# A hybrid decoder block on one core: the order of the mixer's work, with the convolution's mean behind the second pair's state chain, taps of two blocks in turns, and fillers shifted by one place

## The reference, cut to what matters

```
h = rmsnorm(x, norm_mix_g); proj = h @ w_in
u_conv, u_rw, gate_logits = split(proj)

def conv_branch(u, dw, dw_b, ln_g, ln_b, pw, pw_b):
    a, b = split(u, 2); glu = a * sigmoid(b)
    y = depthwise causal convolution of glu, 31 taps, + dw_b
    mean = mean(y); var = mean(square(y - mean))          # over the 512 channels
    yn = silu((y - mean) * rsqrt(var + LN_EPS) * ln_g + ln_b)
    return yn @ pw + pw_b

def rwkv7_branch(u, ...):       # per token: data-dependent decay, delta-rule state 64 x 64 per head
    state = state * w_t + sa * (kk_t * a_t) + v_t * k_t
    y_t = state @ r_t           # then a norm per head, a bonus, an output gate, @ w_o

x = x + (sigmoid(g_conv) * y_conv + sigmoid(g_rw) * y_rw) @ w_out
x = x + peer_ffn(rmsnorm(x, norm_ffn_g), ...)    # product-key experts
return rmsnorm(x, norm_f_g)
```

## Time and profile before

| what | value |
|---|---|
| time, median of 3 runs | 2199.3 us (2196.2 to 2201.05) |
| time of the profiled execution | 2193.65 us |
| its span | 2191.9 us |
| TensorE busy | 2097.6 us, 96% of the span |
| VectorE busy | 1367.6 us, 62% |
| ScalarE busy | 844.4 us, 39% |
| TensorE's granted clock, mean | 0.984 of full speed |

### The profile page before, as it was taken

One profiled execution on the slowest core, in us unless ns is written; L12 is line 12 of the kernel. 1 busy time (PEld: TensorE's weight loads), 2 busy tenths in 40 slices (PEclk: granted clock), 3 DMA queues, 4 the chain that ended last, 5 costly groups with the idle time before them and its releaser, 6 DMA issues.

```text
span 2191.9 us, 37169 instructions
## 1 busy us (share of the span) xinstructions
PE 2097.6 (96%) x12954; PEld 1747.1 (80%) x12954; DVE 1367.6 (62%) x2822; ACT 844.4 (39%) x1196; POOL 375.1 (17%) x463
## 2 busy tenths in 40 slices
PE   5999898997999989999989999999999999999997
PEld 3878786785878878888868888888888888888885
DVE  5478685556999957666645555555555555554555
ACT  4555342533222236666643333323333333333332
POOL 0000000100024539999920000000000000000000
PEclk9999999998999999999999999999999999999998
DMA  4211111342224444555573443443443443453431
GB/s 151 79 59 55 50 55 45 134 160 77 86 92 144 144 144 173 201 201 201 201 244 126 155 155 121 158 153 120 158 153 122 160 156 121 154 161 122 151 101 39
DMA packets 156780, 289.45 MB, mean 132 GB/s; under 512 B 10496, under 2 KB 76160, under 8 KB 154144
## 3 DMA queue, kind: packets, MB, share of 16 engines
q1 hardware_dynamic: 153856, 276.86, 38.1%
q0 software_dynamic: 2848, 11.54, 1.5%
HBM read 231.73 MB, written 56.62 MB: 132 GB/s over the span
## 4 chain that ended last, share of the span: by engine, by line
PE 72%; issue 6%; DVE 1%; DMA 1%; POOL 0%; ACT 0%; DVEq 0%; POOLq 0%; SPq 0%; ACTq 0%
PE unit L350 72%; DMA gl<-g_dram 0%; POOL uL L1995 0%; DMA g_dram<-ge 0%; DVE x L1959 0%; DMA sgw<-gate_dram 0%; DVE rs L1956 0%; PE unit L788 0%; DVE rs L1407 0%; DVE x L1904 0%; DVE aL L1894 0%; DVE af L1889 0%; ACT L954 0%; ACT aH L954 0%; DVE wL L1398 0%
## 5 line engine op out<-in xcount | busy, mean ns | idle before, releaser
L350 PE MATMUL unit<-h2H,uH 128*128 128x512 f32 x1024 | 411.9, 402 | 2.9 <-POOL uL L1995 2.9
L350 PE MATMUL unit<-aH,vH 128*128 128x512 f32 x1024 | 399.6, 390 | 9.3 <-DVE vL L1898 9.3
L350 PE MATMUL unit<-h2H,uL 128*128 128x512 f32 x1024 | 400.3, 391 | 0.0
L350 PE MATMUL unit<-aL,vH 128*128 128x512 f32 x1024 | 399.3, 390 | 0.0
L350 PE MATMUL unit<-h2L,uH 128*128 128x512 f32 x1024 | 399.2, 390 | 0.0
L350 PE MATMUL unit<-aH,vL 128*128 128x512 f32 x1024 | 399.1, 390 | 0.0
L1898 DVE TENSOR_TENSOR vL<-vraw,vH 128x512 fp32r<-128x512 f32 x256 | 176.1, 689 | 236.0 <-ACT vH L954 235.9
L954 ACT ACTIVATE vH<-vraw 128x512 fp32r<-128x512 f32 x256 | 161.0, 630 | 414.8 <-PE unit L350 414.8
L2014 POOL TENSOR_SCALAR oh<-cst,e2s 128x128 f32<-128x128 f32 x384 | 266.3, 710 | 17.5 <-PE unit L350 12.2
L350 PEld LDWEIGHTS unit<-aH,vH 128*128 128x128 f32 x1024 | 192.8, 188 | 49.6 <-DVE vL L1898 9.7
L350 PEld LDWEIGHTS unit<-h2H,uL 128*128 128x128 f32 x1024 | 192.5, 188 | 41.7
(11 more groups left out here) (274 smaller groups left out, 2889.0 us busy)
## 6 DMA issues: line engine op xcount, KB each, us to landing
uraw<-uT SPq DMA_DIRECT2D x128, 512.0 KB, 4.1
vraw<-v_tab SPq DMA_DIRECT2D x256, 256.0 KB, 2.8
wraw<-wall SPq DMA_DIRECT2D x68, 512.0 KB, 3.5
w_dram<-wst SPq DMA_DIRECT2D x16, 2048.0 KB, 6.6
wg<-w_dram SPq DMA_DIRECT2D x32, 1024.0 KB, 6.6
g_dram<-ge SPq DMA_DIRECT2D x64, 256.0 KB, 2.2
gl<-g_dram SPq DMA_DIRECT2D x32, 512.0 KB, 7.6
gate_dram<-gst POOLq DMA_DIRECT2D x16, 256.0 KB, 2.3
```

The costliest lines, as they stand in the source:

```text
L350: return pe.matmul(out, lhsT, rhs, start=start, stop=stop, skip_group_check=True)
```

## The change

The three lists are edited. Low_rank(1) moves from the front of products(0) into the middle of filler 12. The fillers of the first pair's levels are 15 to 19 in place of 16 to 20, that of its transfers 20 in place of 21; 21 is cut and laid around the end of the first chain; token_major(2) stands in front of filler 22. conv_mean moves from the front of solved(2) to behind state_out(2), and conv_square and conv_back move back by one place each. The features of blocks 1 and 3 stand earlier on VectorE; their part that needs the key norms is a function of its own (`key_unit`). Taps are dealt out anew, and their order lets the last 8 taps of one block of channels and the first 8 of the next take turns; a tap waits for the tap before it of its own block.

```
@@ TensorE
-            low_rank(1)
             for k in range(3):
                 products(0, k)
-            whole(12)
+            first_half(12)
+            low_rank(1)
+            second_half(12)
             norm_back(1)
             token_major(0)
             whole(13)
-            whole(14)
             for k in range(3):
                 products(1, k)
-            whole(15)
+            whole(14)
             token_major(1)
             masked_value(0, 1)
...
-            level(0, 16, 0, 1, [(low_rank, 2)])
+            level(0, 15, 0, 1, [(low_rank, 2)])
...
             chain(2)
             products(2, 1)
+            first_half(21)
             chain(3)
             products(2, 2)
             state_out(1)
             norm_back(3)
+            second_half(21)
+            token_major(2)
             whole(22)
-            token_major(2)
             whole(23)
...
             level(4, 29, 2, 3)
-            conv_mean()
             solved(2)
             solved(3)
...
             chain(5)
             state_out(2)
-            conv_square()
+            conv_mean()
             second_half(31)
             chain(6)
             centre(2)
             first_half(32)
             state_out(3)
-            conv_back()
+            conv_square()
             group_square(2)
             centre(3)
             second_half(32)
+            conv_back()
             group_back(2)
             group_square(3)
-            whole(33)
+            first_half(33)
             group_back(3)
+            second_half(33)
@@ VectorE
+            lead = 8
+            tap_order = [(i, j) for _, i, j in sorted((i * (TAPS - lead) + j, i, j) for i in range(CB)
+                                                      for j in range(TAPS))]
...
-                        after(last_tap[0])
+                        after(last_tap[i])
...
             after_fill(28)
+            marks = [ends_diagonal(t) for t in (2, 3)]
+            taps(6)
+            after_fill(29)
+            taps(8)
+            transfers(2, marks[0])
+            transfers(3, marks[1])
+            o_low(1)
             taps(CB * TAPS)
-            marks = [ends_diagonal(t) for t in (2, 3)]
-            after_fill(29)
+            chained(4)
+            after_fill(30)
+            chained(5)
+            state_added(2)
             wait_filled(dve, "cmean")
...
             after_fill(31)
             chained(6)
             state_added(3)
+            wait_taken(dve, "cvar")
+            dve.reciprocal(cdev[:, :], cdev[:, :]).then_inc(cdev_ready, 1)
+            group_inverse(2)
+            after_fill(32)
             wait_filled(dve, "cdev")
```

More of the change, by code:

```diff
@@ L661, in level @@
                 second_half(n)
[L663 to L667, removed]
+            level(0, 15, 0, 1, [(low_rank, 2)])
+            level(1, 16, 0, 1, [(norm_back, 2)])
+            level(2, 17, 0, 1)
+            level(3, 18, 0, 1)
+            level(4, 19, 0, 1)
             solved(0)
@@ L1163, in _ @@
             input_copies(1)
+            after_fill(20)
+            r_scaled(3)
+            exps(3)
             after_fill(21)
[L1165 removed]
+            token_copies(2)
             after_fill(22)
[L1167 to L1168 removed]
             after_fill(23)
@@ L1669, in _ @@
             state_added(1)
+            after_fill(20)
+            key_unit(3)
+            features_a(3)
+            features_b(3)
             after_fill(21)
-            features_a(3)
+            taps(6)
             after_fill(22)
-            features_b(3)
-            taps(4)
-            after_fill(23)
             taps(4)
@@ L1723, in _ @@
             last.then_inc(take_sem("cdev"), 1)
-            group_inverse(2)
-            after_fill(32)
+            group_out(2)
+            group_inverse(3)
             for i in range(2):
@@ L1728, in _ @@
                 tt(cy[:, i, :], cy[:, i, :], csig[:, i, :], ALU.mult).then_inc(cy_swish, 1)
-            group_out(2)
-            group_inverse(3)
+            group_out(3)
+            o_low(2)
             for i in range(2, CB):
```

116 lines of the change are left out of this document (55 added, 61 removed).

## The result

| | before | changed |
|---|---|---|
| device time, median | 2196.39 us (2195.56 to 2201.05, 6 runs) | 2179.82 us (2178.08 to 2181.83, 6 runs) |
| ratio to before | | 0.992, 95% interval 0.9909 to 0.993 |
| span of the profiled execution | 2191.9 us | 2178.0 us |
| mean granted clock of TensorE | 0.984 | 0.985 |

The changed kernel is faster by 16.6 us in the medians and by 13.9 us in the two profiled spans. The forecast was 2181 us, with a range of 2175 to 2190.

What follows compares the result with a forecast made beforehand. TensorE was taken to bound the stretch from 95 to 440 us, with 22.6 us of waits in 2191.9. The terms summed to 17.8, say 18 us, off a 2199.3 us median: 2181 us, range 2175 to 2190.

Steps and rivals of the forecast that it cites:

- mean of the convolution: Moved from before solved(2) to behind chain(5) and state_out(2): the 9.7 us tap wait goes, products run at full clock; +12.0 us.
- aa: Start of the stretch: third product of products(0) no longer finds its PSUM unit held by ScalarE; +2.1 us.
- wait in front of products(1): TensorE waits for block 1's features after the later low_rank(1): 3.2 us where it waited 2.0; -1.2 us.
- chain(3), features(3), masks: Blocks 2 and 3: half of w21 covers chain(3), +2.3; earlier features(3), +3.3; masks in time for transposes, +1.4 us.
- filler 23: Split of w23 queues behind block 3's features on VectorE, ready at 6.3 when w22 ended at 5.7; -0.6 us.
- state_out(3), group_back(3): New waits at the mixer's end: state_out(3) for chained(6), -0.6 us; group_back(3) for group_inverse(3), -0.3 us.
- three fillers cut in two: Fillers 12, 15 and 33 are each split into halves, at 0.2 us each; -0.6 us.
- mixer's gates, and all behind: Weight-split waits after w35: if the 0.6 us wait vanishes, the 1.2 us one grows by as much; 0 us.
- Rival 2: Kinder clock: no half clock behind the new wait before products(1), and small terms turn out kind; 2178 us, chance 0.13.
- Rival 1: VectorE enters level 4 with 4 to 7 us of arrears, so chain(5) waits; gain some 12, 2187 us, chance 0.14.
- Rivals 3 and 4: 3: weight or gate loads hold the mixer's end, 2199 us, 0.05; 4: half clock stays behind products(1), 2204 us, 0.04.
- the 13 that were named as a sign: Sign of being wrong: over 13 us from last gate store to third mixing product, giving gain back after the mixer.

Runs made afterwards that it cites:

- the tail alone: Kernel before with only the end of the mixer in the new order, from level 4 of the second pair on; 2185.85 us, ratio 0.9949.
- four taps later: Changed kernel with four taps moved from behind the diagonals to behind o_low(1), so 15 not 11 lie before chained(4); 2183.36 us, ratio 0.9934.
- the version with low_rank(1) in front: Changed kernel with low_rank(1) back in front of products(0) and filler 12 whole behind them; 2177.21 us, ratio 0.9908.

## Why the prediction was right, point by point

Terms of the sum, forecast and as the two profiled executions have them:

| term | forecast | found |
|---|---|---|
| mean of the convolution | +12.0 | 9.74 + 5.93 - 3.70 = +12.0 |
| aa | +2.1 | +2.1 |
| wait in front of products(1) | -1.2 | 2.0 - 4.6 = -2.6 |
| chain(3), features(3), masks | +7.0 | 2.3 + 3.3 + 1.4 = +7.0 |
| filler 23 | -0.6 | -0.85 |
| state_out(3), group_back(3) | -0.9 | -0.3 - 0.4 = -0.7 |
| three fillers cut in two | -0.6 | -0.6 (not measured apart) |
| mixer's gates, and all behind | 0 | 1.8 - 1.2 = +0.6, less 0.8 = -0.2 |
| clock | 0 | -1.7 at 70 us, -1.7 at 377 us |
| sum | 17.8 | 12.8; the spans say 13.9 |

The one unaccounted microsecond is spread over terms that I did not resolve.

*That 2181 came within 1.2 us of 2179.82 is partly luck.* The gain was forecast too large: 17.8 us, against 16.6 in the medians and 13.9 in the spans. The base was too high as well, and that offset it: 2199.3 us was the median of three runs, over six it is 2196.39, and from there 18 us less is 2178.4. The profiled execution shows it without the medians: 2175.7 was forecast for it, 2179.81 was measured, and w35 was done at 407.9 us and not at 404. What brought the forecast back was the shift of 5.6 us, by which the profiled execution of the kernel before lay below its median; that of the changed kernel lies at its median. With either base the time stays in the range.

*The large term was right in mechanism and size.* The sixteen taps cost TensorE 9.7 us because it had nothing else to do; behind chain(5) their time is covered. The tail alone shows it (11.9 us in the medians, 11.2 by the ratio, 10.4 in the spans), and four later taps show how fine the margin is.

*The step that was mis-sized is "the wait in front of products(1) 2.0 to 3.2, -1.2".* Its working took "6.1 us for gates and scaling" from a stretch of the kernel before, 112.9 to 119.0, that begins behind a table load:

```profile
111.67 1.28 ACT L954 ACT_TABLE_LOAD   x1
```

There the load ran right behind ScalarE's own split, before the stretch that was counted. With low_rank(1) late ScalarE is idle at that place, the load stands behind the wait for the product, and 1.28 us come on top: 14.6 + 1.3 - 11.3 = 4.6, as measured, and 3.24 with the load in front. (The prediction's own 14.6 - 11.3 is 3.3; it wrote 3.2.) The Trainium skill (ScalarE: Activation LUTs, What ACT_TABLE_LOAD costs) counts 1.28 us for the load and some 1.4 more for a drain; here the first part agrees and the second isn't seen, since the next ACTIVATE starts at 120.38, 0.01 us after the load.

*Rival 2 (a kinder clock) did not come.* The half clock followed the new wait in all traces that have it, at 4.6 and at 3.2 us; yet the aa wait of 2.1 us was followed by none in the kernel before and by 3.4 us in the tail alone and in the version with low_rank(1) in front. The wait of 2.04 us for r_in was followed by half clock in the kernel before and by none in the tail alone, and neither the 3.3 us at block 3 (before, the tail alone) nor the 2.95 at chain(5) (four taps later) was followed by any. After a wait of two or three microseconds it can go either way here.

*Rival 1* had its mechanism but not its arrears: VectorE waited for TensorE in front of transfers(3), 2.04 us, and was not late. *Rivals 3 and 4* did not occur. From the third mixing product to the end the two kernels differ by 0.8 us (1757.1 and 1757.9), so hardly any gain was given back, and from the last gate store (408.95) to the third mixing product (420.11) were 11.2 us, under the 13 that were named as a sign.

*The clock was left out of the sum*, and took 3.4 us of it. The stretch at 70 us comes and goes: the kernels with the changed start have 0 us (two traces), 3.4 (eight) or 6.8 (two) there, with the same instructions; the two traces with the start of before had none. Whether the start bears on it, two traces do not show. The longer stretch at 377 belongs to the new tail: every kernel with the new tail had 6.8 us or more between 363 and 390, both with the old one 3.4.

## What to carry to other kernels

A wait with 10 us of another engine's work behind it is best moved behind a chain that needs the same engine little, and the test is one sum: what that engine has left against what the first engine has in front of the new place. Leave more margin than one instruction: here four taps too many cost 3 to 5 us. A producer moved back must be priced with all that its consumer does from idle, a table load among it, and the order of two waits can keep such a load off the path: on ScalarE, write the wait for what comes last first, and the wait for what is long there behind it. Where one product waits for a buffer, cut the piece in front of that product, and do not move the piece that others need early.

## What the runs showed of the hardware

- The table load of ScalarE stands behind or in front of a wait depending on the order in which two waits are written: with the product's wait written last it ran at 119.09 us, behind the product, with it written first at 113.36, in front of it; 1.3 us on the path.
- From 60 to 440 us half clock came in pieces of 3.4, 6.8 and 10.2 us, also with TensorE busy throughout (3.40 of 3.40 us at 70.1), and differed by up to 6.8 us between executions of the same instructions. Two profiled spans cannot be compared to less than about 3 us for that reason alone; the ratios of the medians are not much finer, with intervals of 2.3 to 4.2 us to either side.
- Clear of any wait, half clock came after pieces of some 3.7 us of products with one or eight columns: in all fourteen traces after the sum of squares of the convolution, in ten after that of the key norms.
- Two taps of different blocks in turns start 0.66 to 0.67 us apart, of the same block 0.78, though each is shown with a duration of 0.75.
